# The gate product of three small experts, moved from VectorE to ScalarE and GpSimd

## The reference, cut to what matters

```python
def swiglu(x, w_gate, w_up, w_down):
    return (jax.nn.silu(x @ w_gate) * (x @ w_up)) @ w_down

def moe_swiglu(x, w_router, w_gate, w_up, w_down):
    ...
    for e in range(N_EXPERTS):
        y = y + gates[:, e:e + 1] * swiglu(xt, w_gate[e], w_up[e], w_down[e]).astype(jnp.float32)
```

## Time and profile before

| what | value |
|---|---|
| median of 3 runs | 2023.61 us (2022.56 to 2025.9) |
| profiled execution, its own time | 2025.54 us |
| its span, first to last instruction | 2023.7 us |
| mean granted TensorE clock | 0.994 of full speed |
| PE busy | 1966.3 us (97% of the span) |
| DVE busy | 1506.9 us (74%) |
| ACT busy | 1242.9 us (61%) |
| POOL busy | 83.4 us (4%) |
| small experts, in the span | about 752 to 864, 984 to 1096, 1216 to 1328 us |

### The profile page before, as it was taken

The page is one execution under the profiler, slowest core; times in us unless marked ns, Lnnn a source line. Parts: engine busy times, 40 slices in busy tenths (PEclk is TensorE's granted clock), DMA queues, the critical chain, the costliest instruction groups (busy, mean ns, idle before and its releaser), DMA issues.

```text
span 2023.7 us, 26067 instructions
## 1 busy us (share of the span) xinstructions
PE 1966.3 (97%) x9454; PEld 1634.3 (81%) x9454; DVE 1506.9 (74%) x1579; ACT 1242.9 (61%) x1329; POOL 83.4 (4%) x96
## 2 busy tenths in 40 slices
PE   7999999998999999999999999999899999999998
PEld 6978887888788887788777887778688889798886
DVE  6685546677899999999999899999865556655554
ACT  5555444564777777777777777777644455545443
POOL 0002000000100000000000000020000012000000
PEclk9999999999999999999999999999999999999999
DMA  8348553444999999999999999999755545344550
GB/s 330 118 146 301 208 200 134 162 157 173 391 381 382 362 383 391 406 385 377 391 398 399 370 382 402 391 408 396 254 206 186 190 160 175 138 155 175 188 190 30
DMA packets 79662, 555.13 MB, mean 274 GB/s; under 512 B 8976, under 2 KB 9104, under 8 KB 17632
## 3 DMA queue, kind: packets, MB, share of 16 engines
q1 hardware_dynamic: 73728, 523.01, 67.5%
q0 software_dynamic: 5840, 30.85, 4.1%
HBM read 544.91 MB, written 12.58 MB: 275 GB/s over the span
## 4 chain that ended last, share of the span: by engine, by line
PE 80%; DVE 10%; ACT 5%; issue 4%; DMA 1%; POOL 0%; DVEq 0%; SPq 0%; ACTq 0%
PE ps L604 24%; PE ps L606 24%; PE ps L605 24%; DVE wlo L2096 6%; ACT whi L1579 4%; PE ps L939 1%; DVE probt L2388 1%; PE ps L815 1%; PE ps L1275 0%; PE ps L1251 0%; PE ps L1282 0%; DMA bc<-in_rows 0%; DMA h<-in_route 0%; PE ps L1151 0%; PE ps L1131 0%
## 5 line engine op out<-in xcount | busy, mean ns | idle before, releaser
L2096 DVE TENSOR_TENSOR wlo<-raw,whi 128x2048 fp32r<-128x2048 f32 (+4 forms) x504 | 1137.6, 2261 | 279.3 <-ACT whi L1579 273.3
L1579 ACT ACTIVATE whi<-raw 128x2048 fp32r<-128x2048 f32 (+4 forms) x505 | 949.8, 1883 | 188.3 <-PE ps L606 176.0
L604 PE MATMUL ps<-whi,xth 128*128 128x512 f32 (+3 forms) x1840 | 735.9, 400 | 8.9 <-DVE wlo L2096 5.0
L606 PE MATMUL ps<-whi,xtl 128*128 128x512 f32 (+3 forms) x1840 | 713.4, 388 | 0.0
L605 PE MATMUL ps<-wlo,xth 128*128 128x512 f32 (+3 forms) x1840 | 712.3, 387 | 0.0
L604 PEld LDWEIGHTS ps<-whi,xth 128*128 128x128 f32 x1840 | 348.6, 189 | 80.3 <-DVE wlo L2096 11.8
L606 PEld LDWEIGHTS ps<-whi,xtl 128*128 128x128 f32 x1840 | 347.9, 189 | 68.7
L605 PEld LDWEIGHTS ps<-wlo,xth 128*128 128x128 f32 x1840 | 349.1, 190 | 61.2
L606 PE MATMUL ps<-whi,htl 128*128 128x512 f32 (+2 forms) x580 | 224.8, 388 | 0.0
L604 PE MATMUL ps<-whi,hth 128*128 128x512 f32 (+2 forms) x568 | 221.5, 390 | 1.9 <-DVE wlo L2096 1.8
L605 PE MATMUL ps<-wlo,hth 128*128 128x512 f32 (+2 forms) x568 | 219.4, 386 | 0.0
(11 more groups left out here) (425 smaller groups left out, 1418.7 us busy)
## 6 DMA issues: line engine op xcount, KB each, us to landing
raw<-in_stream SPq DMA_DIRECT2D x475, 1024.0 KB, 6.9
raw<-in_stream SPq DMA_DIRECT2D x16, 768.0 KB, 4.4
bc<-in_rows POOLq DMA_DIRECT2D x4, 1024.0 KB, 6.7
slot_rows<-in_blank POOLq DMA_DIRECT2D x7, 512.0 KB, 10.4
kc<-slot_rows POOLq DMA_DIRECT2D x7, 512.0 KB, 8.3
sum_rows<-r POOLq DMA_DIRECT2D x7, 512.0 KB, 8.8
raw<-in_stream SPq DMA_DIRECT2D x4, 832.0 KB, 6.8
raw<-in_stream SPq DMA_DIRECT2D x4, 640.0 KB, 3.8
```

What stands on the lines that cost most here:

```text
L604: pe.matmul(o, ah, bh, start=start, stop=False, skip_group_check=True)
L606: return pe.matmul(o, al, bh, start=False, stop=stop, skip_group_check=True)
L1579: act.activation(whi[:, c.split, 0:c.width], raw[:, c.raw, 0:c.width], ACT.Copy).then_inc(hi_done, 1)
L2096: dve.tensor_tensor(wlo[:, c.split, 0:c.width], raw[:, c.raw, 0:c.width], f32(whi[:, c.split, 0:c.width]), ALU.subtract).then_inc(lo_done, 1)
```

## The change

In the three small experts ACT, after silu of the gate half into sg[:, 0], copies the up half from PSUM into sg[:, 1] and only then signals; POOL multiplies the two into hfew, a free part of the tile vc, and signals e_h; PE turns hfew in place of hs. DVE's product is left out in these experts. The products stand in POOL's queue between its transfers: two units' products, the store of the expert before, then the other twelve. store(e) no longer waits for its own landing: `outputs` waits for the landing of the store two experts before (y_out), and GpSimd waits for all seven landings once, before it gathers the sums. y_kept is gone. In the branch for an overfull expert ACT raises e_sg so that POOL's waits end there.

```diff
+        hfew = vc[:, :, :, :].rearrange("p t h d -> p (t h d)")[:, 0:FU]
...
                     pool.dma_start(sum_rows[e * P:(e + 1) * P, :], r[:, e % 2, :]).then_inc(sem("y_out"), 16)
-                    pool.wait_ge(sem("y_out"), 16 * (e + 1))
-                    pool.sem_inc(sem("y_kept"), 1)
-
-                pool.sem_inc(sem("y_kept"), 2)
...
+                def products(e, a, b):
+
+                    with pool.Fori(a, b) as it:
+                        pool.wait_ge(sem("e_sg"), it + (U_E * e + 1))
+                        pool.tensor_tensor(hfew, sg[:, 0, :], sg[:, 1, :], ALU.mult).then_inc(sem("e_h"), 1)
+
                 load(1)
-                for e in range(NE - 2):
-                    load(e + 2)
+                for e in range(NE - 1):
+                    if e < NE - 2:
+                        load(e + 2)
+                    if e + 1 in FEW:
+                        products(e + 1, 0, 2)
                     store(e)
-                store(NE - 2)
+                    if e + 1 in FEW:
+                        products(e + 1, 2, U_E)
+                pool.wait_ge(sem("y_out"), 16 * (NE - 1))
                 pool.wait_ge(sem("rt_back"), 1)
...
-                def turn(u):
+                def turn(u, few=False):
                     pe.wait_ge(sem("e_h"), u + 1)
                     for k in range(2):
-                        m = pe.transpose(ps[1][:, k * P:(k + 1) * P], hs[:, 0, k * P:(k + 1) * P], ident)
+                        m = pe.transpose(ps[1][:, k * P:(k + 1) * P], (hfew if few else hs[:, 0])[:, k * P:(k + 1) * P], ident)
...
-                    turn(u)
+                    turn(u, few_now)
...
                 def outputs(e, q, done):
-                    act.wait_ge(sem("y_kept"), e + 1)
+                    if e > 1:
+                        act.wait_ge(sem("y_out"), 16 * (e - 1))
...
-                    act.activation(sg[:, 0, :], ps[0][:, 0:FU], ACT.Silu).then_inc(sem("e_sg"), 1)
+                    if few:
+                        act.activation(sg[:, 0, :], ps[0][:, 0:FU], ACT.Silu)
+                        act.activation(sg[:, 1, :], ps[0][:, FU:2 * FU], ACT.Copy).then_inc(sem("e_sg"), 1)
+                    else:
+                        act.activation(sg[:, 0, :], ps[0][:, 0:FU], ACT.Silu).then_inc(sem("e_sg"), 1)
...
-                act.wait_ge(sem("y_kept"), NE)
+                act.wait_ge(sem("y_out"), 16 * (NE - 2))
...
+                        act.sem_inc(sem("e_sg"), U_MOE)
...
                 def outputs(e, q, done):
-                    dve.wait_ge(sem("y_kept"), e + 1)
+                    if e > 1:
+                        dve.wait_ge(sem("y_out"), 16 * (e - 1))
...
-                    dve.wait_ge(sem("e_sg"), u + 1)
-                    dve.tensor_tensor(hs[:, 0, :], sg[:, 0, :], ps[0][:, FU:2 * FU], ALU.mult).then_inc(sem("e_h"), 1)
+                    if not few:
+                        dve.wait_ge(sem("e_sg"), u + 1)
+                        dve.tensor_tensor(hs[:, 0, :], sg[:, 0, :], ps[0][:, FU:2 * FU], ALU.mult).then_inc(sem("e_h"), 1)
```

## The result

| | before | after |
|---|---|---|
| median of 5 runs | 2023.61 us (2022.47 to 2025.9) | 2034.64 us (2034.42 to 2036.09) |
| profiled execution | 2025.54 us | 2034.6 us |
| its span | 2023.7 us | 2032.7 us |

The ratio is 1.0052, with a 95% interval of 1.004 to 1.0065: 11 us slower, 8 to 13 us by the interval. The profiled executions differ by 9.1 us, because the one of before was 1.9 us above its median.

The account below looks back on a forecast made before the run. The prediction took PE as the bound, waiting in small experts for the product; 9.6 us from 33 units plus 1.2 from six made 10.8 us, added to 2023.6: 2034.4 us, range 2022 to 2042.

Parts of the forecast that it names:

- The bound: Whole kernel: PE, busy for 97% of the span, is the bound; only moving PE's start of some instruction changes the time.
- The price of POOL's product: Small experts: POOL's product waits for DVE's lo, then takes 0.62 us; transposes start 0.29 us later (0.11 to 0.48).
- The faster rival: Small experts: POOL's product slips past a lo, done before PE is there; 5 us faster, 2018.6 us; chance 0.08.
- The sum: Three small experts: 3 x (11 x 0.29 + 2 x 0.2) = 10.8 us slower, added to the median of 2023.6.
- The 33 ordinary units: Eleven units in each of three small experts lose 0.29 us each because the transposes wait for POOL: 9.6 us.
- The first units: First unit of each small expert: PE still has twelve down matmuls and comes to the transposes after POOL; no loss.
- The six with gathered rows: Units 6 and 9 of each small expert, with four extra transposes: later product and later lo of B, 0.2 us each.
- The copy, the waits, the queue: ACT's copy hidden by 0.19 us in usual units; removed landing waits and later loads and stores in POOL's queue cost nothing.
- The short product: Small experts: POOL needs 0.42 us or less behind the lo, sum under 4 us, no change: 2026 us; chance 0.12.
- the second wait: Small experts: POOL's full starting cost or late hi and lo of B, 0.5 us or more a unit; 2043 us; chance 0.08.

Follow-up runs that it names:

- the doubled product: The changed kernel with the product made twice in a row on GpSimd, the first into columns nobody reads: 2060.69 us, ratio 1.0173.
- the two kernels with halves: In small experts, the lo of the next unit's chunk A cut in two: changed kernel 2029.88 us; kernel before, product on VectorE between the halves, 2015.85 us.

## Why the prediction was right

**The bound.** "An engine that is relieved gives nothing by itself" held: what DVE lost in work it gained in waits for ACT, and the waits for the product are what moved the time.

**The price of POOL's product.** The prediction took 0.62 us behind the `lo`; it is 0.60. With 0.05 for the signal in place of 0.06 the transposes were to be 0.29 us later, and are 0.25 (2.17 against 1.92 behind silu). The difference is 0.02 us of the product and 0.01 each of the signal and of the end of the `lo` (1.53 us behind silu before, 1.52 after). The working behind 0.62, a quarter of a longer operation's length plus 0.08 us, was an estimate from four products of another size, with 0.44 and 0.81 as its ends, so that 0.02 us is closer than it could promise. The faster rival took 0.74 us for a product without a `lo`, and 0.74 was measured, but by a slip: its own terms, 0.21 plus 0.55, are 0.76. The later expectation for the doubled product was off too: a second product adds its full 0.72 us, not the 0.55 of one that starts behind a `lo`.

**The sum.** 10.8 us were forecast. Added up from silu to silu over the three small experts of the two traces, it is 9.3 us, and the whole spans differ by 9.0. The 33 ordinary units have 8.6 us of it, 0.26 each, where the forecast had 9.6. The first units have nothing, as forecast. The six with gathered rows have 0.6 us, 0.1 each, where it had 1.2. This is the term whose mechanism was half wrong: the prediction saw both the later product (+0.18, measured 2.25 - 2.08 = 0.17) and the later `lo` of B, and took 0.2 for the two. The runs show that the `lo` of B alone decides there, and that it moves by 0.12 us and not by the copy's 0.28, since before the change ACT already stood idle for a moment between silu and its work on the gathered rows (0.44 us from start to start, where 0.28 would do). The copy alone gave the same 0.1 us a unit. By the medians the change is 11.0 us in its own job, and 10.1 and 9.5 us against the medians of the kernel before in the two later jobs. That 2034.4 and 2034.64 agree to a quarter of a microsecond is luck: the sum was 1.5 us too large, and the medians of the kernel before differ by as much from job to job.

**The copy, the waits, the queue.** The prediction costed them at up to 1.2 us and at nothing. The two kernels that hold the copy and the waits alone gave ratios of 1.0004 and 0.9994. The moved queue was not run by itself without the products; the unchanged large experts are what speaks for its cost of nothing.

**The rivals.** The faster one needed a product that slips past a `lo`. The products of the changed kernel were recorded from 0.74 us behind silu and ended about 0.6 us behind the `lo`. Its other half, that an early product helps, is true: the two kernels with halves have their transposes 1.62 us behind silu, and with the product on VectorE the kernel is faster. With POOL's early product it is 0.24% slower than before, with DVE standing still for it. The short product (0.42 or less) is excluded by 0.60, the second wait by the `lo` of B, which kept 0.46 us to spare (792.75 for 793.21).

## What to carry to other kernels

Before work is moved to a relieved engine, look at when its input is ready and what runs then: here the product waited for a 2.3 us instruction in front of it, and not because VectorE was busy on average; on POOL it waited for the same instruction and then took longer. The cure was to cut the instruction in front, so that the urgent small one goes between its halves, with TensorE waiting for each half: a gain of 0.4% in place of a loss of 0.5%. In this kernel a record on POOL that lies beside a VectorE `lo` (two SBUF inputs) is waiting plus work. Take its length from the end of that instruction, or from a place where VectorE is silent.

## What the runs showed of the hardware

- The same POOL product of 128x256 was recorded with 0.74 us beside an idle DVE, 0.72 directly behind another product, and 1.31 to 1.72 behind a running `lo`, of which 0.58 to 0.62 lie behind its end. So about 0.14 us less is seen behind a `lo` than alone; that part of its start would then be hidden while it waits.
- It blocks in both directions: the `lo` begun at 792.52, while POOL's record runs to 792.83, took 2.46 in place of 2.29 us. The trace of the kernel before has a small product of VectorE that met the last POOL product of the earlier trace rows, which ended at 1695.36; undisturbed it takes 0.22 us:

```profile
1682.95 0.22 DVE L2553 TENSOR_TENSOR cst<-h,rot 128x64 f32<-128x64 f32 x1
...
1694.49 0.94 DVE L2553 TENSOR_TENSOR cst<-h,rot 128x64 f32<-128x64 f32 x1
```

- By the Trainium skill (SBUF — State Buffer, Who interferes with whom) the one that comes second is blocked until the first finishes. The trace agrees on POOL's side: the product's end keeps its distance from the end of the `lo` to 0.04 us in 42 products. On DVE's side the delays are 0.17 us where 0.31 of POOL's record were left, 0.72 where 0.87 were left, and 0.65 where 0.80 were left (the blocked `lo` of the earlier trace rows), always about 0.15 us less than the rest of the record. Either the block ends before POOL's record does, or DVE too hides so much of its start while it waits; no run here tells the two apart.
